# Weighing, rounding and halving two blocks at a time in the second products of a product-key expert layer

## What is computed

```python
u = jnp.take(expert_down, idx, axis=0)
a = jax.nn.gelu(jnp.einsum('nd,nhkd->nhk', xb, u).astype(jnp.float32), approximate=False)
w = (gb * a).astype(xb.dtype)
v = jnp.take(expert_up, idx, axis=0)
return jnp.einsum('nhk,nhkd->nd', w, v)
```

## Time and profile before

| | |
|---|---|
| median of three executions | 1588.9 us (1587.73 to 1590.93) |
| the profiled execution | 1593.95 us |
| its span, from first to last instruction | 1591.9 us |
| mean granted clock of TensorE | 0.997 |
| second products, first to last matmul | 1077.6 to about 1580 us of the span |

### The profile page before, as it was taken

How to read it: one execution, slowest core, us unless ns; L and a number is a source line. 1 busy time by engine, 2 the same in 40 slices (tenths; PEclk the granted TensorE clock), 3 DMA queues, 4 the chain that set the end, 5 groups by cost and what they waited for, 6 DMA issues and landing times.

```text
span 1591.9 us, 26152 instructions
## 1 busy us (share of the span) xinstructions
PE 1569.8 (99%) x9939; PEld 1485.6 (93%) x9939; DVE 1165.7 (73%) x2254; ACT 666.0 (42%) x996; POOL 994.0 (62%) x562
## 2 busy tenths in 40 slices
PE   8999999999999999999999999999999999999997
PEld 6888888888989999999999999999999999999997
DVE  4155361342479999999999983337999999999994
ACT  5352442542434444444444444333434333333333
POOL 4463376433145799887777778876766766665621
PEclk9999999999999999999999999999999999999999
DMA  5232242323423999988999999969999999999981
GB/s 186 93 101 72 69 157 93 107 65 106 153 86 116 289 351 353 329 290 305 378 413 391 403 415 385 343 237 375 410 410 410 408 401 406 398 401 411 396 336 54
DMA packets 131425, 441.80 MB, mean 278 GB/s; under 512 B 14080, under 2 KB 29440, under 8 KB 123008
## 3 DMA queue, kind: packets, MB, share of 16 engines
q1 hardware_dynamic: 61168, 228.88, 39.6%
q0 software_dynamic: 46080, 167.79, 27.6%
q10 hardware_dynamic: 24080, 43.85, 7.2%
HBM read 396.65 MB, written 43.25 MB: 276 GB/s over the span
## 4 chain that ended last, share of the span: by engine, by line
PE 56%; DVE 1%; DMA 1%; issue 0%; POOL 0%; ACT 0%; ACTq 0%; DVEq 0%
PE psum L1541 17%; PE psum L1543 17%; PE psum L1542 17%; PE psum L1828 4%; DMA kept<-up_in,kept 1%; DVE arena L1209 0%; DVE arena L1282 0%; DVE arena L1342 0%; POOL w_low L462 0%; DVE psum L1205 0%; PE psum L1864 0%; POOL arena L539 0%; PE psum L1858 0%; ACT arena L985 0%; PE psum L1848 0%
## 5 line engine op out<-in xcount | busy, mean ns | idle before, releaser
L462 POOL TENSOR_TENSOR w_low<-kept,w_high 128x1024 fp32r<-128x1024 f32 x212 | 520.1, 2457 | 304.1 <-ACT w_high L592 301.9
L1541 PE MATMUL psum<-hT_high,w_high 128*128 128x352 f32 (+2 forms) x1408 | 484.5, 344 | 3.2 <-POOL w_low L462 3.1
L1542 PE MATMUL psum<-hT_low,w_high 128*128 128x352 f32 (+2 forms) x1408 | 476.7, 339 | 0.0
L1543 PE MATMUL psum<-hT_high,w_low 128*128 128x352 f32 (+2 forms) x1408 | 476.6, 339 | 0.0
L1541 PE MATMUL psum<-wgt_high,up_high 128*128 128x352 f32 x1016 | 328.6, 323 | 1.9 <-DVE wgt_low L1444 1.8
L1543 PE MATMUL psum<-wgt_high,up_low 128*128 128x352 f32 x1016 | 330.2, 325 | 0.0
L1542 PE MATMUL psum<-wgt_low,up_high 128*128 128x352 f32 x1016 | 328.7, 323 | 0.0
L1541 PEld LDWEIGHTS psum<-hT_high,w_high 128*128 128x128 f32 x1408 | 264.7, 188 | 17.4 <-issue 2.9
L592 ACT ACTIVATE w_high<-kept 128x1024 fp32r<-128x1024 f32 x212 | 223.7, 1056 | 134.0 <-PE psum L1543 90.7
L1543 PEld LDWEIGHTS psum<-hT_high,w_low 128*128 128x128 f32 x1408 | 264.8, 188 | 12.7
L1542 PEld LDWEIGHTS psum<-hT_low,w_high 128*128 128x128 f32 x1408 | 265.0, 188 | 12.1 <-issue 0.5
(11 more groups left out here) (273 smaller groups left out, 1967.5 us busy)
## 6 DMA issues: line engine op xcount, KB each, us to landing
kept<-down_in SPq DMA_DIRECT2D x128, 512.0 KB, 6.5
arena<-up_pairs SPq DMA_DIRECT2D x64, 1024.0 KB, 11.0
kept<-front_w SPq DMA_DIRECT2D x92, 512.0 KB, 3.6
gate_dram<-arena ACTq DMA_DIRECT2D x40, 512.0 KB, 10.9
arena<-hid_dram SPq DMA_DIRECT2D x56, 352.0 KB, 14.1
arena<-gate_dram SPq DMA_DIRECT2D x8, 1280.0 KB, 14.8
kept<-gate_dram SPq DMA_DIRECT2D x8, 1280.0 KB, 16.2
hid_dram<-arena ACTq DMA_DIRECT2D x56, 176.0 KB
```

The lines of the kernel that those rows point to most:

```text
L462: nc.gpsimd.tensor_tensor(lower, ring[:, p % RING, :], high.bitcast(F32), ALU.subtract).then_inc(low_ready, 1)
L1541: nc.tensor.matmul(out, lhs[0], rhs[0], start=first, stop=False)
L1542: nc.tensor.matmul(out, lhs[0], rhs[1], start=False, stop=False)
L1543: return nc.tensor.matmul(out, lhs[1], rhs[0], start=False, stop=last)
```

## The change

Two blocks are weighed in one pair of instructions (2 x 320 columns and 2 x 32), rounded in one (2 x 352) and halved in one (2 x 352). The kept activations move so that the two blocks of a pair stand at a fixed distance (`kept_pair`). VectorE's order becomes, for an even u: `low_up(u)`, `weigh(u + 2)` for blocks u + 2 and u + 3, `sparse_ups(u)`, `weights_low(u)` for blocks u and u + 1, `low_up(u + 1)`, `sparse_ups(u + 1)`; at u = 0 `weights_low(0)` stands ahead of `weigh(2)`. ScalarE rounds the pair ahead of `high_up` of its odd block. The wait for the stored activations moves from the last kept block to the one two before, and POOL's wait ahead of row 6 asks for four weighed blocks instead of three.

```diff
@@ -248,7 +248,11 @@
         hot_i = at(205.5, TB * P // 2).bitcast(BF16).rearrange("p (n i r) -> p n i r", n=PAIRS, r=2)
         stage = at(140, 2 * P * CH, 2, P, CH)
         near = at(172, P * NEAR, P, NEAR)
-        hid_kept = [at(kb, DE) for kb in [156 + 1.5 * j for j in range(10)] + [133, 134.375, 135.75, 114, 205.5, 138]]
+        hid_kept = [at(kb, DE) for kb in [156 + 1.5 * j for j in range(10)] + [133 + 1.375 * j for j in range(4)] + [114, 138.5]]
+
+        def kept_pair(j):
+            first, apart = (156 + 3 * j, 1.5) if j < 5 else (133 + 2.75 * (j - 5), 1.375) if j < 7 else (114, 24.5)
+            return at(first, int(2 * apart * KB), 2, int(apart * KB))[:, :, 0:DE]
 
 
         uraw = at(76, RING_U * D, RING_U, D)
@@ -532,7 +536,7 @@
                 if UP_FIRST <= k < RING_C:
                     pool.wait_ge(up_done, k - UP_FIRST + 1)
                 if UP_FIRST + 2 <= k < RING_C:
-                    pool.wait_ge(w_raw, 2 * (3 if k == UP_FIRST + 2 else 6))
+                    pool.wait_ge(w_raw, 2 * (4 if k == UP_FIRST + 2 else 6))
                 if k >= RING_C:
                     pool.wait_ge(sparse_added, k - RING_C + 1)
                 numbers = edge_idx[:, k:k + 1] if k < EDGE_SLOTS else idx3[:, k - EDGE_SLOTS:k - EDGE_SLOTS + 1]
@@ -595,9 +599,9 @@
                 act.wait_ge(ld_up[s // 2], landed)
                 nc.scalar.activation(up_hi[:, s % 4, :], uraw[:, up_slot(s), :], ACT.Copy).then_inc(up_high, 1)
 
-            def weight_high(i, s):
-                act.wait_ge(w_raw, i * 2 + 2)
-                nc.scalar.activation(wgt_half[0][:, s, 0:DE], wraw[:, s, 0:DE], ACT.Copy).then_inc(w_high, 1)
+            def weights_high(i, s):
+                act.wait_ge(w_raw, i * 2 + 4)
+                nc.scalar.activation(wgt_half[0][:, s:s + 2, 0:DE], wraw[:, s:s + 2, 0:DE], ACT.Copy).then_inc(w_high, 1)
 
             def ahead(b):
 
@@ -920,7 +924,7 @@
                 i = SPILL + j
                 if j == 0:
                     act.wait_ge(stored[0], 16 * PIECES * ((FAR + 1) // 2))
-                if j == KEEP - 1:
+                if j == KEEP - 3:
                     for s in range(2):
                         act.wait_ge(hid_stored[s], 16 * (SPILL // HIDS))
                 if i + 2 < NK:
@@ -930,25 +934,26 @@
                 if i == NK - 4:
                     act.wait_ge(dot_done, ROWS)
                     high_up(0, 0, 16)
-                    weight_high(0, 0)
+                    weights_high(0, 0)
                 if i == NK - 3:
                     act.wait_ge(dot_done, ROWS)
                     nc.scalar.activation(gel3, dot3, ACT.Gelu).then_inc(gel3_ready, 1)
                 if i == NK - 2:
                     high_up(1, 1, 16)
-                    weight_high(1, 1)
-            for s in range(2, 4):
-                high_up(s, s, 16)
-                weight_high(s, s)
+            high_up(2, 2, 16)
+            weights_high(2, 2)
+            high_up(3, 3, 16)
             for u in range(4, RING_U):
                 act.wait_ge(up_done, u - 3)
+                if u % 2:
+                    weights_high(u - 1, (u - 1) % 4)
                 high_up(u, u, 16)
-                weight_high(u, u % 4)
             with act.Fori(1, NK // RING_U) as r:
                 for s in range(RING_U):
                     act.wait_ge(up_done, r * RING_U + (s - 3))
+                    if s % 2:
+                        weights_high(r * RING_U + (s - 1), (s - 1) % 4)
                     high_up(r * RING_U + s, s, r * 16 + 16)
-                    weight_high(r * RING_U + s, s % 4)
 
             act.preload_act_table_set("natural_log_exp_and_others")
             act.wait_ge(sparse_added, UP_ROWS)
@@ -1422,47 +1427,49 @@
                 for k in range(UP_ROWS * (u - 1) // (NK - 4), min(UP_ROWS, UP_ROWS * u // (NK - 4))):
                     sparse_up(k)
 
-            def weigh(i, landed, block, kept_hid=None):
+            def weigh(i, block):
+                s, both = i % 4, hidr[:, i % (2 * PAIRS_IN):i % (2 * PAIRS_IN) + 2, :]
+                if i >= 4:
+                    dve.wait_ge(w_ready, i - 2)
+                dve.wait_ge(ld_gate[i // GT % 2], 16 * (i // GT // 2 + 1))
+                if i < KEEP:
+                    both = kept_pair(i // 2)
+                    dve.wait_ge(gelu_out, block + 4)
+                else:
+                    dve.wait_ge(ld_hid[i // 2 % PAIRS_IN], 16 * ((i - KEEP) // 2 // PAIRS_IN + 1))
+                nc.vector.tensor_tensor(
+                    wraw[:, s:s + 2, 0:FAR * CH].rearrange("p a (c n) -> p a c n", n=CH),
+                    both[:, :, 0:FAR * CH].rearrange("p a (c n) -> p a c n", n=CH),
+                    gates[i // GT % 2][:, :, i % GT * CH:(i % GT + 2) * CH].rearrange("p c (a n) -> p a c n", n=CH), ALU.mult)\
+                    .then_inc(w_raw, 2)
+                nc.vector.tensor_tensor(wraw[:, s:s + 2, FAR * CH:DE], both[:, :, FAR * CH:DE], near[:, block:block + 2, :],
+                                        ALU.mult).then_inc(w_raw, 2)
+
+            def weights_low(i):
                 s = i % 4
-                dve.wait_ge(ld_gate[i // GT % 2], 16 * (i // GT // 2 + 1))
-                if kept_hid is None:
-                    dve.wait_ge(ld_hid[i // 2 % PAIRS_IN], 16 * ((i - KEEP) // 2 // PAIRS_IN + 1))
-                else:
-                    dve.wait_ge(gelu_out, landed)
-                h = hidr[:, i % (2 * PAIRS_IN), :] if kept_hid is None else kept_hid
-                nc.vector.tensor_tensor(
-                    wraw[:, s, 0:FAR * CH].rearrange("p (c n) -> p c n", n=CH),
-                    h[:, 0:FAR * CH].rearrange("p (c n) -> p c n", n=CH),
-                    gates[i // GT % 2][:, :, i % GT * CH:(i % GT + 1) * CH], ALU.mult).then_inc(w_raw, 1)
-                nc.vector.tensor_tensor(
-                    wraw[:, s, FAR * CH:DE].rearrange("p (i n) -> p i n", i=1),
-                    h[:, FAR * CH:DE].rearrange("p (i n) -> p i n", i=1),
-                    near[:, block:block + 1, :], ALU.mult).then_inc(w_raw, 1)
-
-            def weight_low(i, s):
-                dve.wait_ge(w_high, i + 1)
-                nc.vector.tensor_tensor(wgt_half[1][:, s, 0:DE], wraw[:, s, 0:DE], wgt_half[0][:, s, 0:DE].bitcast(F32),
-                                        ALU.subtract).then_inc(w_ready, 1)
+                dve.wait_ge(w_high, i // 2 + 1)
+                nc.vector.tensor_tensor(wgt_half[1][:, s:s + 2, 0:DE], wraw[:, s:s + 2, 0:DE],
+                                        wgt_half[0][:, s:s + 2, 0:DE].bitcast(F32), ALU.subtract).then_inc(w_ready, 2)
 
             dve.wait_ge(gate_out, 2 * STEPS + 3)
             step.end()
-            weigh(0, SPILL + 3, SPILL, hid_kept[0])
-            for s in range(KEEP - 1):
-                low_up(s, s % RING_U)
-                weigh(s + 1, SPILL + s + 4, SPILL + s + 1, hid_kept[s + 1])
-                weight_low(s, s % 4)
-                if s == 0:
+            weigh(0, SPILL)
+            for u in range(0, NK, 2):
+                low_up(u, u % RING_U)
+                if u == 0:
+                    weights_low(u)
+                if u + 2 < NK:
+                    weigh(u + 2, u + 2 + SPILL if u + 2 < KEEP else u + 2 - KEEP)
+                if u == 0:
                     dve.wait_ge(gel3_ready, 1)
                     step(nc.vector.tensor_tensor(w3, gel3, gate3, ALU.mult))
                 else:
-                    sparse_ups(s)
-            for u in range(KEEP, NK):
-                low_up(u - 1, (u - 1) % RING_U)
-                weigh(u, None, u - KEEP)
-                weight_low(u - 1, (u - 1) % 4)
-                sparse_ups(u - 1)
-            low_up(NK - 1, RING_U - 1)
-            weight_low(NK - 1, 3)
+                    if u < NK - 2:
+                        sparse_ups(u)
+                    weights_low(u)
+                low_up(u + 1, (u + 1) % RING_U)
+                if u < NK - 2:
+                    sparse_ups(u + 1)
 
             def scaled(t):
                 for c in (slice(0, 512), slice(512, D)):
```

## The result

The changed kernel is slower by a third to half of a per cent. The medians of six executions each are 1595.97 and 1588.76 us, 7.2 us or 0.45% apart; the ratio on record is lower, 1.0034 with a 95% interval of 1.0019 to 1.0050, which is 5.4 us (3.0 to 7.9). The profiled execution took 1595.90 us, its span is 1593.9 us.

A forecast was written before the change was run, and what follows sets the result against it. The prediction took TensorE as the bound, with VectorE and the DMA engines just behind. It summed 1.8 + 0.8 + 0.2 = +2.8, say +3 us, onto 1588.9 for 1591.9 us; own range 1588.5 to 1593, overall 1587 to 1600.

The forecast's parts named there:

- VectorE's 13 us: Pairing saves VectorE 0.2 us a pair, 13 us over 64 pairs, worth nothing in the even part.
- rivals 2 and 3: Faster outcomes: clean start of the second products, 1585.1 us, chance 0.07; VectorE setting the pace, 1575.9 us, chance 0.03.
- rival 3: VectorE sets the pace, so its saved 13 us come through: 1575.9 us, chance 0.03; sign: matmuls under 0.161 us apart.
- The new order is what counts: VectorE's even-block low half now stands behind its own expert rows, making TensorE wait at blocks 4, 8 and 28.
- No change, from its upper side: Whole kernel: about +3 us, to 1591.9 us, within the 0.2% (3.2 us) a measurement can tell.
- rival 1: Second products starve more than once, with clock falls: +9.2 us, to 1598.1 us; chance 0.44.
- the one at block 52: Second products: a TensorE wait with the clock down again there, as at block 28, would indicate rival 1.
- Block 4: TensorE waits 2.8 us for the low half behind late row 4, plus 1.6 us of lower clock.
- Block 8: TensorE waits 1.1 us for the low half behind row 9, taken as too short to lower the clock.
- Block 28: TensorE waits 0.8 us because spilled activations are wanted one block earlier; bounds 0 and 2.6 with the lower clock.
- POOL's `low(127)`: End of the first products: later rounding and subtraction cost 0 by the rows, 0.2 us added, bounds 0 and 0.6.
- The rule on the port: VectorE and GpSimd lock each other out for whole instructions; could push low(127) to 1074.4, the sum up by 0.6 us.

The follow-up runs named there:

- e10: Kernel before the change, with the 160 expert rows spread over blocks 3 to 125, two blocks later at the start: ratio 0.9999 (0.9989 to 1.0009).
- e11: e3 with the 160 expert rows spread over blocks 3 to 125: ratio to the kernel before 0.9998 (0.9985 to 1.0012).
- e1: Kernel before the change, run again unchanged for a second profile: ratio 0.9997 (0.9986 to 1.0009), profiled execution 1590.58 us.
- e2: Changed kernel with weights_low of the pair ahead of the even block's expert rows instead of behind: ratio to before 1.0013 (1.0003 to 1.0023).
- e3: e2 with the next pair's weighing also moved behind up_low of the odd block: ratio to before 1.0004 (0.9993 to 1.0015).
- e4: Changed kernel's order with every paired instruction split into two single-block ones: ratio to before 1.0023 (1.0009 to 1.0037).
- e9: Changed kernel run again unchanged, for a second profile and ratio: 1.0038 (1.0023 to 1.0053) to the kernel before.
- e5: Changed kernel with every fourth spilled pair's load ahead of the gate load in SP's queue: ratio to before 1.0019 (1.0008 to 1.0030).
- e12: Changed kernel with the 160 expert rows spread over blocks 3 to 125: ratio to before 1.0011 (1.0000 to 1.0021).
- e7: Kernel before the change with the expert rows spread over blocks 9 to 124: ratio 0.9992 (0.9981 to 1.0003).
- e6: Changed kernel with the 160 expert rows spread over blocks 9 to 124 instead of 1 to 124: ratio to before 1.0024 (1.0012 to 1.0037).
- e8: e3 with the expert rows spread over blocks 9 to 124: ratio to the kernel before 1.0009 (0.9997 to 1.0021).

## Why the prediction was right or wrong, point by point

**TensorE is the bound, and VectorE's 13 us are worth nothing: right.** VectorE's busy time fell by 12.8 us and nothing came of it; rivals 2 and 3, the faster ones, did not happen. VectorE's share behind block 8 fell to 410.13 of 443.70 us, 92%, where I had said about 93%. e10 against e11 shows the same without any wait in the way. My sign for rival 3, matmuls less than 0.161 us apart, did appear, 0.160 from block 29 on; but the kernel before does that as well in e1 (last section), so the sign did not tell the two apart.

**The new order is what counts, at blocks 4, 8 and 28: right.** In the first profile all three waits stand where the hand calculation put them, with the late instruction it named. e2, e3 and e4 show that the order makes those at 4 and 28; a wait at block 8 stands in e1, e2 and e3 as well, and the order only moved it. The spilled pair of block 30 was weighed at 1188.25, against a forecast of 1188.1.

**"No change, from its upper side": wrong in size.** The forecast of +3 us is a ratio of 1.0019, the lower end of the first interval and below the second. The measured 1595.97 us lies outside the forecast's own range (to 1593) and nearer to the 1598.1 of rival 1, to which 0.44 had been given. Of rival 1's signs, the wait with its fall at block 28 came and the one at block 52 did not. Term by term, from the first profile and e9:

- Block 4, forecast 2.8 us and 1.6 of lower clock: 1.15 us with no fall in the one, 3.65 us with a fall in the other. The term holds as a middle; that it does is luck, for it took one landing as fixed. In the first, row 4 landed 0.8 us sooner than in the profile of before (1092.96 against 1093.77).
- Block 8, forecast 1.1: 2.1 us in the one, none in the other, where TensorE came there later.
- Block 28, forecast 0.8 with bounds of 0 and 2.6: 2.3 us and 1.6 of lower clock, 3.9 in all and over the bound. This is the term that was mis-sized. The pair landed as foreseen and `wgt_low` ended 0.3 us late; but TensorE was ready for block 28 at 1190.4, not at 1191.7, since block 4 had cost it 1.15 us instead of 4.4. The delay that I carried forward to shorten this wait was mostly not there, so what the sum had too much at block 4 came back here, and the clock fell as well. In e9, which lost 5.2 us at block 4, no wait came at 28 but one of 2.05 us at block 20, which the sum did not hold: I followed one late pair, while VectorE waited for ten to twelve of them (29.1 us in the first profile).
- POOL's `low(127)`, forecast 0.2 with bounds 0 and 0.6: 0 in both profiles of the changed kernel, but 0.3 in e5, 0.7 in e4, 0.9 in e3 and 1.2 in e12, where the same lines run. The bound was too narrow. Ahead of it stands VectorE's first weighing, which waits for the first load of gates: until 1068.46 and 1067.30 in the two profiles of the changed kernel, but 1068.92, 1069.98 and 1069.20 in e4, e3 and e12. The sum took that landing as fixed.

The sum of waits and lower clock was forecast at 2.8 + 1.6 + 1.1 + 0.8 = 6.3 us; the two profiles have 7.2 and 7.3 (3.65 + 1.6 + 2.05). Against 3.8 and 4.1 in the two profiles of before that is 3.1 to 3.5 us of the 5.4 us that the ratio stands for (3.0 to 7.9; the medians lie 7.2 apart). The rest is not settled: profiles hold one execution each, and the last section shows a spread of that size in TensorE's pace.

**The base of the sum.** The forecast was added to the median of before, which was sound; the profiled execution of before was 3.4 us longer than e1's, not for its waits but for its pace, and 0.6 us of it for a later start of the stage.

**The reading of the clock.** From a mean of 0.54 I read that half of the time is spent at the lower level. With levels of 1.2 and 2.4 GHz, 0.5 and 1.0 of full speed, it is nine tenths of that window. The price of 1.6 us was read from the starts and is not touched by this.

**The rule on the port.** I put the Trainium skill's rule (SBUF — State Buffer, section "SBUF: two separate sides") at 0.6 us for `low(127)`. e12 shows it in rows of VectorE, POOL and TensorE:

```profile
1072.75 2.40 DVE L1445 TENSOR_TENSOR arena<-arena 128x64 f32<-128x64 f32 x1
```

```profile
1072.02 3.05 POOL L466 TENSOR_TENSOR w_low<-kept,w_high 128x1024 fp32r<-128x1024 f32 x1 [5.59 <-ACT w_high L596]
```

```profile
1075.21 0.40 PE L1548 MATMUL psum<-hT_high,w_high 128*128 128x352 f32 x1 [1.18 <-POOL w_low L466]
```

VectorE's 64-wide weighing takes 2.40 us instead of 0.22 while POOL subtracts, and POOL 3.05 instead of 2.40 behind VectorE's weighing of 640; the two end and begin in turn. The trace agrees with a lock that one holds for a whole instruction. The changed kernel's two profiles have the same: in the first, the weighing took 2.43 us and POOL 3.08, and `low(127)`, 0.5 us late at its start, ended at 1074.36, where the sum had put 1073.6 and the rule 1074.4; it cost nothing there because TensorE came to it only at 1074.62. In e3 POOL took 2.38 us, so that e3's 0.9 us are a late start and not the lock.

## What to carry to other kernels

When one engine has no gap in a stage, fewer instructions on another buy nothing; look instead at what the merging does to the order, since a merged step has to wait for the later of its inputs and hands both results on late. In an engine's queue, put work that the bound engine waits for ahead of work that itself waits for a DMA (e2), and ask of every step that moves earlier whether its data, too, come earlier. Where the DMA engines are full, wanting a load later can move a wait as well as remove it: in e7, e10 and e11 the waits went, in e6, e8 and e12 others came.

## What the runs showed that I had not expected

**TensorE has two even paces.** With no wait and the clock at 1.00, a block of 24 matmuls takes 3.867 us in some stretches and 3.840 in others. Before, first profile, and e1, the same kernel, over the same 360 us:

```profile
1200.00:1560.00 360.00, 360.00 (x2236) 360.00 (x2235) 344.55 (x500) 137.70 (x187) 215.38 (x114) 1.00 0.98 387
```

```profile
1200.00:1560.00 360.00, 360.00 (x2252) 360.00 (x2251) 345.21 (x501) 140.52 (x190) 209.42 (x114) 1.00 0.97 386
```

2236 matmuls against 2252, with TensorE busy throughout; over the 119 blocks behind block 8 this is 0.027 x 119 = 3.2 us. Every profile of this case begins the second products at the slower pace, and many changes, either way, stand at a wait of TensorE, some as short as 0.1 us: e1 and e2 change to the faster pace at block 8 and keep it; the changed kernel changes at block 4, back at block 6, and at block 28 for good; the first profile of before changes at block 5 and back at block 8, and e5 at 4 and back at 6; these two and e3 kept the slower pace behind block 8, although they waited there and the clock fell too. Others have no wait that I can see: in e9 two blocks behind its wait at block 20, in e8 at blocks 78 and 94, there and back, in e6 at block 94 and later, in e7 at block 118. e10 and e11, with no wait at all, kept the slower pace to the end. From the first to the last matmul of the stage the two profiles of before take 502.4 and 499.6 us, those of the changed kernel 503.5 and 502.8; the waits, the falls of the clock and the two paces account for these differences to 0.2 us. What the waits of e9 cost against the first profile of before, its faster pace gave back. So taking out the wait at block 8 (4 us) forfeits, in part of the executions, a gain of 3 us that such a wait sometimes brings, which fits the ratios of e10, 0.9999, and e7, 0.9992, where the waits alone would have made 0.9975. That this is what ate the gain is argued from a few profiles, not shown, and what sets the pace stays open.

**The clock falls after some waits and not after others of the same length.** 2.1 us before block 8 of the changed kernel left it at 1.00, 2.0 us in the earlier trace rows took it to 0.54, 2.4 us before block 6 of e12 left it alone. My line, "the wait of 0.2 us did not, the one of 2.0 did", was too simple a rule for pricing it.

No version measured here beats the kernel before beyond its interval; the nearest is e7 at 0.9992.
